# A PEER layer's first gathered rows brought into the query projection, with seven buffers that are free there

## The chip, the cores and the metric

The kernel runs on one core of one Trainium2 chip. The metric is device time in microseconds, the median of several runs. TensorE, VectorE, ScalarE, GpSimd and SyncE each run their own instruction stream and are ordered by semaphores alone; sixteen DMA engines move data between HBM and SBUF.

## The reference, cut to what matters

The program is two blocks on 256 tokens of width 2048 in float32. The first is a gated convolution with attention, the second a convolution and state-space mixer followed by a PEER layer (product-key retrieval of single-neuron experts) and a last norm. The change concerns the PEER layer:

```python
def peer(h, w_q, sub_keys, u_tab, v_tab):        # blocks of 128 tokens
        q = (xb @ w_q).reshape(128, 8, 2, 128)
        s = jnp.einsum('thcd,hcnd->thcn', q, sub_keys)
        s_top, i_top = lax.top_k(s, 16)
        cand = s_top[:, :, 0, :, None] + s_top[:, :, 1, None, :]
        best, pos = lax.top_k(cand.reshape(128, 8, 256), 16)
        expert = jnp.take_along_axis(cand_idx, pos, axis=-1)   # row of 16384
        gates = jax.nn.softmax(best, axis=-1)
        act = jax.nn.gelu(jnp.einsum('td,thkd->thk', xb, u_tab[expert]))
        return jnp.einsum('thk,thkd->td', gates * act, v_tab[expert])
```

Each token picks 8 heads x 16 = 128 experts, so each block of 128 tokens reads 128 x 128 rows of 2048 floats (8 KB) from each of two tables.

## The kernel before, in words

Everything ahead of PEER is a chain of projections. SyncE loads weight slabs of 1 MB into four buffers `weight_raw` (`load`, L276), each after the tile that last read the buffer, so four slabs ahead. TensorE multiplies tile by tile (`tile`, L381; `split_product`, L399, which uses the copies `weight_high`, `weight_low` and the operands `o_high`, `o_low` that lie over `operand`), and ScalarE or VectorE reads each tile out of PSUM.

**Query projection** (TensorE L618 to L629, ScalarE L907 to L914). Sixteen tiles, each 16 k-steps of two passes, from `op_b`. After each of tiles 0 to 3 TensorE turns four blocks (`M_TOK`, four transposes each, L622 to L627), which ScalarE copies out (L912): blocks 0 to 7 are the residual, into `y_tok`, and 8 to 15 the normed h, into `h_tok`. Two PSUM banks serve them in turn (`misc_bank`, L420). After the tiles of `SCORE_AFTER` (4, 5, 6, 8, 10, 12, 14, 15) TensorE makes one head's scores against the sub-keys (`head_scores`, L608), which ScalarE copies to `x_f` (`scores_out`).

**Picks** (VectorE). `head_picks` (L1417) finds the 16 best of each half, the 256 sums and the 16 best of these. `experts` (L1428) turns the positions of several heads into table rows and raises `picks_ready`; for block 0 it comes after heads 0 to 3, 4 to 6 and 7 (`HEAD_PARTS`). `softmax` (L1451) makes the gates, with the exponential on ScalarE (`softmax_exp`).

**Gathers** (GpSimd, L351 to L372). One indirect DMA brings one pick of 128 tokens: 128 rows of 8 KB, 1 MB, into one of eight buffers `rows` (two of `weight_raw`, six in `slots`; L202). GpSimd issues them in order: block 0's 128 of table u, its 128 of v, then block 1's, 512 in all, in rounds of eight buffers. Each waits until its buffer has been used (`row_free`), and the first for the last head's scores and the end of the projection (L362, L363).

**Dots and sums.** For table u VectorE multiplies each row with `h_tok` and adds it up (`dot_rows`, L1474). Then ScalarE makes the gelu and VectorE the weights `pick_w`. For table v the buffers with an odd number go to VectorE, which adds weight times row to `y_tok` (`add_rows`, L1489), and those with an even number to TensorE (L644), which multiplies them by a diagonal that ScalarE writes (L929), four products of 512 columns into PSUM. `add_sums` (L1493) joins both. `finish` (L1500) waits for ScalarE's square and root (L935, L937), scales by the gain, and SyncE stores (L320). VectorE picks block 1's heads in block 0's rounds of sums; block 1's `experts` and `softmax` stand ahead of the last round (L1515). The order on VectorE is written out at L1461 to L1466 and L1511 to L1527:

```python
            dot_rows(0)
            for i in range(ROUNDS):
                if i == ROUNDS - 1:
                    experts(1, 0, PEER_H)
                    softmax(1)
                if i < PEER_H:
                    head_picks(1, i)
                add_rows(0, i)
            add_sums(0)
            finish(0)
            dot_rows(1)
```

Of the kernel before, what the change touches and what calls it, by code (L numbers as in the profile page):

```python
# [33 lines left out]
HEAD_PARTS = ((0, 4), (4, 7), (7, 8))  # L34
SCORE_AFTER = [4, 5, 6, 8, 10, 12, 14, 15]
PICKS = PEER_H * PEER_K

# [83 lines left out]
def build(nc, d):  # L121
    ctx = ExitStack()
    with ctx:  # L123
# [7 lines left out]
        with nc.sbuf_tensor("weight_low", [P, NSLAB, SLAB], F32R) as w_low, \  # L131
                nc.sbuf_tensor("operand_low", [P, KD, T], F32R) as o_low, \
                nc.sbuf_tensor("operand_high", [P, KD, T], F32R) as o_high:
            pass
        w_raw = sb("weight_raw", [P, NSLAB, SLAB])
        opnd = sb("operand", [P, 2, KD, T])
        w_high = sb("weight_high", [P, NHIGH, SLAB], F32R)
# [64 lines left out]
        rows = [w_raw[:, n, :] for n in range(2)] + [slots_f[:, n * D:(n + 1) * D] for n in range(6)]  # L202
        ROWS = len(rows)
        ROUNDS = PICKS // ROWS
        PE_AT = range(0, ROWS, 2)
        DVE_AT = range(1, ROWS, 2)

# [50 lines left out]
        M_TOK = M_SUB + 4  # L258
        M_S = M_TOK + 16
# [67 lines left out]
        def _(pool):  # L327
# [23 lines left out]
            def gather(rnd, col0, table):  # L351

                for n in range(ROWS):
                    pool.wait_ge(row_free[n], rnd + 1)
                    nc.gpsimd.indirect_dma_start(  # L355
                        rows[n], None, table, bass.IndirectOffsetOnAxis(ap=picks[:, col0 + n:col0 + n + 1], axis=0),
                    ).then_inc(gathered[n], 16)

            for n in range(ROWS):
                pool.sem_inc(row_free[n], 1)  # L360

            pool.wait_ge(misc_done, M_S + PEER_H)  # L362
            pool.wait_ge(proj_done, TILES)  # L363
            per_head = PEER_K // ROWS
            for t in range(TT):
                for v, table in ((0, d["peer_u_2"][0]), (1, d["peer_v_2"][0])):
                    parts = [(*heads, n + 1) for n, heads in enumerate(HEAD_PARTS)] if t == v == 0 \
                        else [(0, PEER_H, len(HEAD_PARTS) + t)]
                    for first, last, ready in parts:
                        pool.wait_ge(picks_ready, ready)  # L370
                        for i in range(first * per_head, last * per_head):
                            gather(i + (2 * t + v) * ROUNDS, i * ROWS + t * PICKS, table)  # L372

# [4 lines left out]
        def _(pe):  # L378
# [229 lines left out]
            def head_scores(h):  # L608

                pe.wait_ge(proj_freed, freed(TILE_WQ + 2 * h + 2))  # L610
                bank = misc_bank(M_S + h, h == 0)
# [5 lines left out]

            pe.wait_ge(proj_freed, freed(TILE_WQ))  # L618
            for n in range(16):
                tile(TILE_WQ, n, op_b, ready=(lambda k: (h_scaled, 2 * KD + k + 1)) if n == 0 else None)  # L620

                for u in range(4 * n, 4 * n + 4 if n < 4 else 4 * n):  # L622
                    bank = misc_bank(M_TOK + u, u == 0)
                    src, t, g = (x_t, op_b)[u // 8], (u // 4) % 2, u % 4
                    for j in range(4):
                        tr = nc.tensor.transpose(bank[:, j * P:(j + 1) * P], src[:, 4 * g + j, t * P:(t + 1) * P], ident[:, :])
                    tr.then_inc(misc_done, 1)  # L627
# [5 lines left out]
            pe.wait_ge(misc_freed, M_S + 8)  # L633
            for t in range(TT):
# [4 lines left out]
                for i in range(ROUNDS):  # L639
                    for j, n in enumerate(PE_AT):  # L640
                        pe.wait_ge(diag_ready, (ROUNDS * t + i) * len(PE_AT) + j + 1)
                        pe.wait_ge(gathered[n], (i + (2 * t + 1) * ROUNDS + 1) * 16)
                        for c in range(4):
                            mm = nc.tensor.matmul(ps_v[:, c, :], diag[:, n, :], rows[n][:, c * 512:(c + 1) * 512],  # L644
                                                  start=False, stop=False, skip_group_check=True)
                        mm.then_inc(row_free[n], 1)
# [9 lines left out]
        def _(act):  # L656
# [244 lines left out]
            def scores_out(h):  # L901
                m = M_S + h
# [3 lines left out]

            for n in range(16):  # L907
                read_out(TILE_WQ, n, slot(n))
                for u in range(4 * n, 4 * n + 4 if n < 4 else 4 * n):
                    act.wait_ge(misc_done, M_TOK + u + 1)  # L910
                    dst, t, g = (y_tok, h_tok)[u // 8], (u // 4) % 2, u % 4
                    act_copy(dst[:, t, 512 * g:512 * g + 512], ps_m[:, (M_TOK + u) % 2, :]).then_inc(misc_freed, 1)  # L912
                if n in SCORE_AFTER:
                    scores_out(SCORE_AFTER.index(n))  # L914

# [5 lines left out]
            for t in range(TT):  # L921
# [3 lines left out]
                for i in range(ROUNDS):  # L925
                    for n in PE_AT:
                        at = i * ROWS + t * P + n
                        act.wait_ge(row_free[n], i + (2 * t + 1) * ROUNDS + 1)
                        nc.scalar.activation(diag[:, n, :], ident[:, :], ACT.Copy,  # L929
                                             scale=pick_w[:, at:at + 1]).then_inc(diag_ready, 1)  # L930
                if t == 0:
                    softmax_exp(1)
# [4 lines left out]
                nc.scalar.activation(out_sd[:, t:t + 1], out_ss[:, t:t + 1], ACT.Sqrt, bias=eps_c, scale=1.0 / D).then_inc(out_rooted, 1)  # L937

# [4 lines left out]
        def _(dve):  # L943
# [473 lines left out]
            def head_picks(t, h):  # L1417
                dve.wait_ge(misc_freed, M_S + h + 1)
# [42 lines left out]
            for h in range(PEER_H):  # L1461
                head_picks(0, h)
                for first, last in HEAD_PARTS:
                    if h == last - 1:
# [89 lines left out]
```

## Time and profile before

| | |
|---|---|
| median of 3 runs | 2709.89 us (2707.55 to 2713.97) |
| profiled execution, its span | 2704.8 us (it shows no other time of its own) |
| TensorE busy | 1845.0 us (68%) |
| VectorE busy | 1824.7 us (67%) |
| GpSimd busy | 903.3 us (33%) |
| ScalarE busy | 467.2 us (17%) |
| moved by DMA | 747.27 MB, of it 536.90 MB by the gathers |
| mean granted TensorE clock | 0.863 of full speed |

A slice of the page is a fortieth of the span, 67.6 us. The query projection lies at about 1271 to 1399 us and the gathers at 1401 to 2692. In the rows, PE is TensorE, PEld its weight load, DVE VectorE, ACT ScalarE, POOL GpSimd and SP SyncE; x16 is a count of instructions, and the brackets at a row's end hold the engine's idle time before it and what ended that.

### The profile page before, as it was taken

To read this page: it belongs to the slowest core of one execution; us is meant where nothing else is said; L and a number is where in the kernel's file an instruction comes from. 1 tells how busy PE (TensorE), PEld (TensorE's weight loads), DVE (VectorE), ACT (ScalarE), POOL (GpSimd) and SP (SyncE) were. 2 spreads that over 40 slices of the span, in tenths; PEclk is the share of its full clock that TensorE was granted. 3 is DMA by queue.
4 is the path that set the end of the run, shared out by engine and by line. 5 is a ranking of instruction groups with operands and counts; after the bars stand their busy time and mean duration, and the time that the engine had idled before them with its cause. 6 is when DMAs were issued, how large, how long until landed. Compare 5 with 4: busy or idle time off the path is not lost. (4 is left out here: it accounts for less than half of the span.)

```text
span 2704.8 us, 25287 instructions
## 1 busy us (share of the span) xinstructions
PE 1845.0 (68%) x9428; PEld 1434.6 (53%) x9428; DVE 1824.7 (67%) x2603; ACT 467.2 (17%) x737; POOL 903.3 (33%) x541
## 2 busy tenths in 40 slices
PE   7999999999999999999970000377772000067776
PEld 6999999987878888898860000122221000022222
DVE  5665676516868977254269999877449999954444
ACT  4345555401020101233110000000010000000001
POOL 2000000000000000000018888665556888855553
PEclk8999999998989999999995555699997555589999
DMA  6655555653535554465449999999999999999998
GB/s 161 186 166 162 166 162 156 172 140 105 148 91 156 140 155 141 140 187 155 126 149 422 422 422 422 422 421 421 422 422 382 422 422 422 421 422 422 422 421 338
DMA packets 458283, 747.27 MB, mean 276 GB/s; under 512 B 22130, under 2 KB 391236, under 8 KB 392260
## 3 DMA queue, kind: packets, MB, share of 16 engines
q0 software_dynamic: 73728, 536.90, 47.8%
q1 hardware_dynamic: 373248, 207.63, 27.2%
q10 hardware_dynamic: 11204, 1.29, 0.4%
q8 instruction: 74, 1.21, 0.2%
q14 instruction: 29, 0.24, 0.0%
HBM read 743.68 MB, written 2.10 MB: 276 GB/s over the span
## 5 line engine op out<-in xcount | busy, mean ns | idle before, releaser
L395 PE MATMUL ps<-operand,weight_raw 128*128 128x256 f32 x3072 | 674.7, 382 | 6.4 <-DVE operand L981 5.9
L395 PEld LDWEIGHTS ps<-operand,weight_raw 128*128 128x128 f32 x3072 | 588.1, 192 | 90.0 <-issue 8.4
L644 PE MATMUL ps<-weight_raw,residual_t 128*128 128x512 f32 x256 | 123.5, 627 | 677.2 <-ACT residual_t L929 637.4
L1474 DVE SCALAR_TENSOR_TENSOR slots<-slots,work 128x2048 f32<-128x2048 f32 x192 | 437.5, 2291 | 30.3 <-DMA slots<-in_peer_u,slots 29.9
L644 PEld LDWEIGHTS ps<-weight_raw,residual_t 128*128 128x128 f32 x256 | 48.2, 198 | 752.6 <-ACT residual_t L929 699.9
L644 PE MATMUL ps<-slots,residual_t 128*128 128x512 f32 x768 | 353.2, 603 | 119.0 <-DMA slots<-in_peer_v,slots 119.0
L355 POOL DMA_INDIRECT slots<-in_peer_u,slots x192 | 395.5, 2060 | 61.9 <-issue 58.6
L413 PE MATMUL ps<-operand_high,weight_high 128*128 128x256 f32 x1536 | 389.2, 293 | 10.5 <-POOL operand_low L337 6.4
L414 PE MATMUL ps<-operand_low,weight_high 128*128 128x256 f32 x1536 | 378.8, 286 | 0.0
L348 POOL IOTA slots<- 128x16 f32 x1 | 0.1, 146 | 1127.1 <-DVE operand L1387 1127.1
L1489 DVE SCALAR_TENSOR_TENSOR work<-slots,work 128x2048 f32<-128x2048 f32 x96 | 225.7, 2351 | 221.6 <-DMA slots<-in_peer_v,slots 221.2
L970 DVE TENSOR_TENSOR weight_low<-weight_raw,weight_high 128x2048 fp32r<-128x2048 f32 x96 | 220.6, 2298 | 159.2 <-ACT weight_high L658 158.6
L355 POOL DMA_INDIRECT slots<-in_peer_v,slots x192 | 261.6, 1362 | 183.8 <-PE ps L644 147.5
L644 PEld LDWEIGHTS ps<-slots,residual_t 128*128 128x128 f32 x768 | 139.1, 190 | 332.7 <-ACT residual_t L929 169.2
L413 PEld LDWEIGHTS ps<-operand_high,weight_high 128*128 128x128 f32 x1536 | 298.7, 194 | 17.9 <-issue 10.1
L414 PEld LDWEIGHTS ps<-operand_low,weight_high 128*128 128x128 f32 x1536 | 299.6, 195 | 2.2 <-issue 1.9
L355 POOL DMA_INDIRECT weight_raw<-in_peer_u,slots x64 | 133.6, 2087 | 273.0 <-PE ps L614 228.4
L658 ACT ACTIVATE weight_high<-weight_raw 128x2048 fp32r<-128x2048 f32 x96 | 183.2, 1909 | 116.5 <-PE ps L417 99.0
L417 PE MATMUL ps<-operand_high,weight_low 128*128 128x256 f32 x1536 | 201.6, 284 | 0.2 <-DVE weight_low L970 0.2
L417 PEld LDWEIGHTS ps<-operand_high,weight_low 128*128 128x128 f32 x1536 | 192.7, 193 | 0.4 <-DVE weight_low L970 0.4
L1474 DVE SCALAR_TENSOR_TENSOR weight_raw<-weight_raw,work 128x2048 f32<-128x2048 f32 x64 | 146.1, 2291 | 9.2 <-DMA weight_raw<-in_peer_u,slots 9.1
L711 ACT ACTIVATE slots<-ps 128x256 f32<-128x256 f32 x136 | 52.3, 384 | 563.1 <-PE ps L395 356.3
(209 smaller groups left out, 1508.8 us busy)
## 6 DMA issues: line engine op xcount, KB each, us to landing
weight_raw<-in_w_in SPq DMA_DIRECT2D x120, 1024.0 KB, 6.1
weight_raw<-in_w_out SPq DMA_DIRECT2D x32, 1024.0 KB, 5.9
weight_raw<-in_peer_w_q SPq DMA_DIRECT2D x16, 1024.0 KB, 5.8
weight_raw<-in_ssm_w_val SPq DMA_DIRECT2D x8, 1024.0 KB, 5.3
weight_raw<-in_ssm_w_gate SPq DMA_DIRECT2D x8, 1024.0 KB, 5.3
weight_raw<-in_conv_w_out SPq DMA_DIRECT2D x8, 1024.0 KB, 5.3
slots<-in_peer_u,slots POOLq DMA_INDIRECT x192, 16.4
slots<-in_peer_v,slots POOLq DMA_INDIRECT x192, 15.9
```

What stands on the lines that cost most here:

```text
L348: nc.gpsimd.iota(iota16, pattern=[[1, 16]], base=0, channel_multiplier=0, allow_small_or_imprecise_dtypes=True).then_inc(zero_ready, 1)
L355: nc.gpsimd.indirect_dma_start(rows[n], None, table, bass.IndirectOffsetOnAxis(ap=picks[:, col0 + n:col0 + n + 1], axis=0),).then_inc(gath ...
L395: mm = nc.tensor.matmul(ps_p[:, t % PSLOTS, :], w[:, k, :], operand[:, k, :], start=(k == order[0]), stop=(k == order[-1]))
L413: nc.tensor.matmul(out, high[:, k, :], o_high[:, k, :], start=(k == order[0]), stop=False)
L414: nc.tensor.matmul(out, high[:, k, :], o_low[:, k, :], start=False, stop=False)
L417: mm = nc.tensor.matmul(out, low[:, k, :], o_high[:, k, :], start=False, stop=(k == order[-1]))
L644: mm = nc.tensor.matmul(ps_v[:, c, :], diag[:, n, :], rows[n][:, c * 512:(c + 1) * 512], start=False, stop=False, skip_group_check=True)
L658: return nc.scalar.activation(dst, src, ACT.Copy)
L711: return nc.scalar.activation(dst, ps_p[:, n % PSLOTS, :], func, **kw).then_inc(proj_freed, 1)
L970: v.tensor_tensor(w_low[:, s % NSLAB, :], w_raw[:, s % NSLAB, :], w_high[:, i % NHIGH, :], ALU.subtract).then_inc(w_low_ready, 1)
L1474: v.scalar_tensor_tensor(out=rows[n], in0=rows[n], scalar=1.0, in1=h_tok[:, t, :], op0=ALU.mult, op1=ALU.mult, accum_out=dots[:, at:at + 1 ...
L1489: v.scalar_tensor_tensor(out=y_tok[:, t, :], in0=rows[n], scalar=pick_w[:, at:at + 1], in1=y_tok[:, t, :], op0=ALU.mult, op1=ALU.add).then ...
```

## The change

- `HEAD_PARTS` is now head 0, heads 1 to 3, heads 4 to 7; head 0's scores follow tile 1 and head 1's tile 4.
- TensorE turns blocks 0 to 7 ahead of tile 0, and the other eight two by two after tiles 1, 2, 3 and 5.
- There are eleven row buffers. Seven are free during the query projection: two in the place of `weight_high` (which now lies over a buffer `rows_high`), two in `op_a`, three in `slots`; the first 28 gathers go round in these. From gather 28 on, which waits for the end of the projection, the four of `weight_raw` join. `ROW[s]` and `USES[s]` are worked out for each of the 512 gathers, and the semaphore waits count by them.
- After `head_picks` of heads 0 to 6 VectorE dots 3, 4, 3, 3, 4, 3 and 4 rows, 24 in all (`DOTS_AFTER`), and the other 104 after `softmax(0)`.
- In block 0's sums VectorE picks head h of block 1 after pick 8h + 7, and makes `experts(1)` at pick 71. `softmax(1)` and `finish(0)` move into block 1's dots, after dots 12 and 8. On ScalarE `softmax_exp(1)` moves behind block 0's square and root.
- Odd and even go by pick and not by buffer, and the diagonals take sixteen places in turn.

```diff
-HEAD_PARTS = ((0, 4), (4, 7), (7, 8))
-SCORE_AFTER = [4, 5, 6, 8, 10, 12, 14, 15]
+HEAD_PARTS = ((0, 1), (1, 4), (4, 8))
+SCORE_AFTER = [1, 4, 6, 8, 10, 12, 14, 15]
+DOTS_AFTER = [3, 4, 3, 3, 4, 3, 4]
 PICKS = PEER_H * PEER_K
+EARLY_ROWS, MORE_ROWS = 7, 4
+ROWS = EARLY_ROWS + MORE_ROWS
+EARLY_PICKS = 4 * EARLY_ROWS
+def row_of(s):
+    if s < EARLY_PICKS:
+        return s % EARLY_ROWS
+    return (EARLY_ROWS + s - EARLY_PICKS) % ROWS
+ROW = [row_of(s) for s in range(4 * PICKS)]
+USES = [ROW[:s].count(ROW[s]) for s in range(4 * PICKS)]
...
-        rows = [w_raw[:, n, :] for n in range(2)] + [slots_f[:, n * D:(n + 1) * D] for n in range(6)]
-        ROUNDS = PICKS // ROWS
-        PE_AT = range(0, ROWS, 2)
-        DVE_AT = range(1, ROWS, 2)
+        rows_a = op_a.rearrange("p a b -> p (a b)")
+        rows = [rows_high[:, n, :] for n in range(2)] + [rows_a[:, n * D:(n + 1) * D] for n in range(2)] \
+            + [slots_f[:, n * D:(n + 1) * D] for n in range(3, 6)] + [w_raw[:, n, :] for n in range(MORE_ROWS)]
...
+            return (8, 9) if n == 1 else (10, 11) if n == 2 else (12, 13) if n == 3 else (14, 15) if n == 5 else ()
...
-            pool.wait_ge(misc_done, M_S + PEER_H)
-            pool.wait_ge(proj_done, TILES)
+            def gather(s, col, table):
+                b = ROW[s]
+                if USES[s] > 0:
+                    pool.wait_ge(row_free[b], USES[s])
+                nc.gpsimd.indirect_dma_start(
+                    rows[b], None, table, bass.IndirectOffsetOnAxis(ap=picks[:, col:col + 1], axis=0),
+                ).then_inc(gathered[b], 16)
             for t in range(TT):
...
+                        for i in range(first * PEER_K, last * PEER_K):
+                            s = (2 * t + v) * PICKS + i
+                            if s == EARLY_PICKS:
+                                pool.wait_ge(proj_done, TILES)
+                            gather(s, t * PICKS + i, table)
...
             pe.wait_ge(proj_freed, freed(TILE_WQ))
+            for u in range(8):
+                tokens(u)
             for n in range(16):
                 tile(TILE_WQ, n, op_b, ready=(lambda k: (h_scaled, 2 * KD + k + 1)) if n == 0 else None)
+                for u in tokens_after(n):
+                    tokens(u)
                 if n in SCORE_AFTER:
                     head_scores(SCORE_AFTER.index(n))
...
+                for i in range(0, PICKS, 2):
+                    if i >= 32:
+                        before = (2 * t + 1) * PICKS + i - 32
+                        act.wait_ge(row_free[ROW[before]], USES[before] + 1)
+                    nc.scalar.activation(diag[:, i // 2 % 16, :], ident[:, :], ACT.Copy,
+                                         scale=pick_w[:, t * P + i:t * P + i + 1]).then_inc(diag_ready, 1)
-                if t == 0:
-                    softmax_exp(1)
                 nc.scalar.activation(small[:, 52:53], eps_c, ACT.Sqrt)
...
+                if t == 0:
+                    softmax_exp(1)
...
+            done = 0
+            for h in range(PEER_H):
+                head_picks(0, h)
+                for first, last in HEAD_PARTS:
+                    if h == last - 1:
+                        experts(0, first, last)
+                if h < len(DOTS_AFTER):
+                    if h == 0:
+                        dve.wait_ge(misc_freed, M_TOK[11] + 1)
+                    for i in range(done, done + DOTS_AFTER[h]):
+                        dot_row(0, i)
+                    done += DOTS_AFTER[h]
+            softmax(0)
+            for i in range(done, PICKS):
+                dot_row(0, i)
+            weigh(0)
+
+            for i in range(1, PICKS, 2):
+                add_row(0, i)
+                if i % 8 == 7 and i // 8 < PEER_H:
+                    head_picks(1, i // 8)
+                elif i == 8 * PEER_H + 7:
+                    experts(1, 0, PEER_H)
+            add_sums(0)
+            sums_ready()
+            for i in range(PICKS):
+                if i == 8:
+                    finish(0)
+                elif i == 12:
+                    softmax(1)
+                dot_row(1, i)
+            weigh(1)
+            for i in range(1, PICKS, 2):
+                add_row(1, i)
+            add_sums(1)
+            sums_ready()
+            finish(1)
```

`dot_row(t, i)` and `add_row(t, i)` hold one turn each of the loops in the old `dot_rows` and `add_rows`, `weigh` the end of the old `dot_rows`, and `sums_ready` the first line of the old `finish`.

## Rows read from the trace of the kernel before

**Rows 1.** The page: GB/s of the 40 slices, and the gathers' DMA queue.

```profile
GB/s 161 186 166 162 166 162 156 172 140 105 148 91 156 140 155 141 140 187 155 126 149 422 422 422 422 422 421 421 422 422 382 422 422 422 421 422 422 422 421 338
...
q0 software_dynamic: 73728, 536.90, 47.8%
```

**Rows 2.** Windows: us, busy PE, PEld, DVE, ACT, POOL, granted clock, DMA share, GB/s.

```profile
1480.00:1600.00 120.00, 0.00 (x0) 0.00 (x0) 111.62 (x99) 0.00 (x0) 105.07 (x50) 0.50 1.01 422
...
1800.00:2000.00 200.00, 147.04 (x321) 57.49 (x320) 115.18 (x140) 16.06 (x40) 110.41 (x81) 1.00 1.01 422
```

**Rows 3.** Waits, 1250 to 2710: us in total, times, longest.

```profile
DVE slots L1408 <- ACT residual_t L658: 73.3, 7, 41.5
```

**Rows 4.** Windows of 2 us at the edges of the gathers.

```profile
1402.00:1404.00 2.00, 2.00 (x6) 0.83 (x5) 1.93 (x3) 0.44 (x1) 1.63 (x2) 1.00 0.63 168
...
2040.00:2042.00 2.00, 1.35 (x4) 0.28 (x2) 1.97 (x2) 0.00 (x0) 0.00 (x0) 1.00 0.31 131
...
2688.00:2690.00 2.00, 0.79 (x2) 0.49 (x3) 1.03 (x1) 0.00 (x0) 0.00 (x0) 1.00 0.41 172
```

**Rows 5.** Timeline of the query projection: start us, us, engine, line, operation.

```profile
1270.89 9.04 PE L395 MATMUL ps<-operand,weight_raw 128*128 128x256 f32 x32 [2.96 <-DVE operand L981]
...
1279.77 1.04 PE L626 MATMUL ps<-ident,residual_t 128*128 128x128 f32 x8
...
1281.75 1.08 ACT L658 ACTIVATE work<-ps 128x512 f32<-128x512 f32 x2 [0.26 <-PE ps L626]
...
1282.03 7.07 PE L395 MATMUL ps<-operand,weight_raw 128*128 128x256 f32 x32
...
1317.57 0.60 ACT L658 ACTIVATE residual_t<-ps 128x512 f32<-128x512 f32 x1 [0.51 <-PE ps L614]
...
1346.99 0.38 ACT L711 ACTIVATE slots<-ps 128x256 f32<-128x256 f32 x1 [6.52 <-PE ps L395]
...
1398.91 0.38 ACT L711 ACTIVATE slots<-ps 128x256 f32<-128x256 f32 x1 [6.31 <-PE ps L395]
```

**Rows 6.** Window of 1 us in tile 0; the last three columns as in rows 2.

```profile
1273.00:1274.00 1.00, 1.00 (x3) 0.75 (x3) 1.00 (x4) 0.00 (x0) 0.00 (x0) 0.50 0.00 0
```

**Rows 7.** Timeline of VectorE: picks, table rows, softmax and first dots.

```profile
1354.32 0.20 DVE L1434 TENSOR_SCALAR slots<-slots 128x64 uint32<-128x64 uint32 x1
...
1362.67 0.23 DVE L1448 SCALAR_TENSOR_TENSOR slots<-slots 128x64 uint32<-128x64 f32 x1
...
1405.27 0.48 DVE L1408 MAX8 slots<-residual_t 128x8 f32<-128x128 f32 x2
...
1411.02 0.37 DVE L1434 TENSOR_SCALAR slots<-slots 128x16 uint32<-128x16 uint32 x1
...
1414.59 0.28 DVE L1455 TENSOR_TENSOR slots<-slots 128x128 f32<-128x128 f32 x1
...
1416.14 2.29 DVE L1474 SCALAR_TENSOR_TENSOR weight_raw<-weight_raw,work 128x2048 f32<-128x2048 f32 x1
...
1418.36 2.29 DVE L1474 SCALAR_TENSOR_TENSOR weight_raw<-weight_raw,work 128x2048 f32<-128x2048 f32 x1
```

**Rows 8.** Timeline of GpSimd: the first gather and the eighth.

```profile
1400.79 1.32 POOL L355 DMA_INDIRECT weight_raw<-in_peer_u,slots  x1 [228.45 <-PE ps L614]
...
1410.46 0.94 POOL L355 DMA_INDIRECT slots<-in_peer_u,slots  x1 [0.30 <-issue]
```

**Rows 9.** Line 355, all gathers: from issue to landing.

```profile
DMA to landing us min/median/max: 5.7/16.3/17.5
```

**Rows 10.** The page's DMA issues: KB each, us to landing.

```profile
weight_raw<-in_peer_w_q SPq DMA_DIRECT2D x16, 1024.0 KB, 5.8
```

**Rows 11.** DMA queues in 1298 to 1316, two weight loads: records, MB, share.

```profile
q1 hardware_dynamic: 4128, 2.10, 43.2%
```

**Rows 12.** DMA queues in 2065 to 2071, gathers (q0) and the store (q1).

```profile
DMA packets 455, 2.55 MB, mean 425 GB/s; under 512 B 38, under 2 KB 38, under 8 KB 249
...
q0 software_dynamic: 228, 1.69, 66.6%
q1 hardware_dynamic: 227, 0.86, 35.1%
```

More of the change, by code:

```diff
@@ L638, in _ @@
                     nc.tensor.matmul(ps_v[:, c, :], zero_row[:, 0:P], zero_row, start=True, stop=False, skip_group_check=True)
[L639 to L646, printed above, removed]
+                for i in range(0, PICKS, 2):
+                    s = (2 * t + 1) * PICKS + i
+                    b = ROW[s]
+                    pe.wait_ge(diag_ready, (t * PICKS + i) // 2 + 1)
+                    pe.wait_ge(gathered[b], 16 * (USES[s] + 1))
+                    for c in range(4):
+                        mm = nc.tensor.matmul(ps_v[:, c, :], diag[:, i // 2 % 16, :], rows[b][:, c * 512:(c + 1) * 512],
+                                              start=False, stop=False, skip_group_check=True)
+                    mm.then_inc(row_free[b], 1)
                 for c in range(4):
@@ L1459, in softmax, with dot_row, weigh @@
                 own.do(v.tensor_tensor(g, g, head_rs.unsqueeze(2).broadcast_to([P, PEER_H, PEER_K]), ALU.mult))
[L1461 to L1464, printed above, removed]
-                        experts(0, first, last)
-            softmax(0)
-            def dot_rows(t):
-                for i in range(ROUNDS):
-                    for n in range(ROWS):
-                        at = i * ROWS + t * P + n
-                        dve.wait_ge(gathered[n], (i + 2 * t * ROUNDS + 1) * 16)
-                        v.scalar_tensor_tensor(out=rows[n], in0=rows[n], scalar=1.0, in1=h_tok[:, t, :], op0=ALU.mult,
-                                               op1=ALU.mult, accum_out=dots[:, at:at + 1]).then_inc(row_free[n], 1)
-                for n in range(ROWS):
-                    dve.wait_ge(row_free[n], (2 * t + 1) * ROUNDS + 1)
+            def dot_row(t, i):
+                s = 2 * t * PICKS + i
+                b, at = ROW[s], t * P + i
+                dve.wait_ge(gathered[b], 16 * (USES[s] + 1))
+                v.scalar_tensor_tensor(out=rows[b], in0=rows[b], scalar=1.0, in1=h_tok[:, t, :], op0=ALU.mult,
+                                       op1=ALU.mult, accum_out=dots[:, at:at + 1]).then_inc(row_free[b], 1)
+            def weigh(t):
+                for b in range(ROWS):
+                    dve.wait_ge(row_free[b], uses_before(b, (2 * t + 1) * PICKS))
                 v.tensor_copy(small[:, 48:49], small[:, 0:1]).then_inc(dots_ready, PICKS)
```

96 lines of the change are left out of this document (40 added, 56 removed).

## The prediction

> **What bounds the kernel now.** I read the page's slices and queues first [rows 1]: from the 22nd slice on the DMA engines move 422 GB/s almost without a pause, against 91 to 187 before it, and the gathers' queue carries 536.90 MB. Then the stages [rows 2]: in the dots (1480 to 1600) and in the sums (1800 to 2000) the DMA share is 1.01, while VectorE is busy for 112 of 120 and 115 of 200 us and TensorE for 0 and 147. So the second half is bound by bytes: 512 gathers of 536.90/512 = 1.0486 MB at 422 GB/s, 2.485 us each, 1272.3 us in all. No engine's work there is worth time; only bytes moved earlier, and pauses of the DMA engines, are. Both exist ahead of it: VectorE stands 73.3 us for scores in the projection [rows 3], and GpSimd 228.45 us before its first gather [rows 8].
>
> The fine windows [rows 4] give the edges. Row data starts near 1402.7 (share 0.63 in 1402 to 1404) and ends near 2688.9 (0.41 in 2688 to 2690): 1286.2 us. The rows take 1272.3; the last gain (1 MB) and block 0's store (1 MB), by their bytes, 2.5 us each; that leaves some 9 us of pause, most of it at the block boundary, where block 1's picks come late (share 0.31 in 2040 to 2042). From the last byte to the span's end it is 2704.8 - 2688.9 = 15.9 us, the last sum, the norm and the store, which the change leaves as they are.
>
> The span, 2704.8 us, is all that the profiled execution gives of its own time; the median of the runs is 5.1 us above it. All sums are made against the span, and 5.1 is added at the end. A measurement tells some 0.2% (5.4 us) from no change.
>
> **1. Turned blocks.** Eight of the sixteen now stand ahead of tile 0, where TensorE waits 2.96 us for the scaled operand [rows 5]. ScalarE, free after its root, copies a pair out per 1.35 us (1.09 and a wait of 0.26), so the four pairs take until about 1273. Tile 0 then starts 2 us later than before. But it took 9.04 us there, at a granted clock of 0.50 (1.2 GHz) in 1273 to 1274 [rows 6] after that wait, and a plain tile takes 6.9 (0.38 and a wait of 6.52): it ends near 1280 as before. The other eight come in pairs after tiles 1, 2, 3 and 5 at 1.04 us a pair, where two pairs, with the wait for ScalarE, took 2.26 (1279.77 to 1282.03). Four groups at 2.3 become four at 1.04: 5 us less. The last read-out, at 1398.9 before, would come at 1394.
>
> **2. Head 0's picks.** Its scores follow tile 1, so they are copied out at 1280 + 6.9 + 1.0 + 1.5 = 1289.4 (1.5 from the read-out at 1316.68 to the end of the copy at 1318.17). One head's picks take 5.75 us (1405.27 to 1411.02) and the table rows of 16 picks 3.57 (to 1414.59) [rows 7]: GpSimd starts gathering at 1298.7, 102 us sooner [rows 8]. The blocks of h_tok that the dots read (tokens 8 to 11) are out by 1298, so waiting for them costs nothing. A gather is issued per 1.24 us (0.94 and 0.30) and lands 5.7 us after its issue at the least [rows 9].
>
> **3. Rows against weights.** The query weights are loaded meanwhile, 5.8 us from issue to landing [rows 10], four slabs ahead, that is 4 x 6.9 = 27.6 us before TensorE needs one: 21.8 us of slack. Two loads are 4128 records and 43.2% of 18 us [rows 11]: 129 records per engine, 3.9 us, 0.03 us a record. A gathered row is 8 records per engine of 0.31 us. How do two queues share an engine? No stretch has such loads beside gathers; the nearest is block 0's store (4 KB records) among gathers: 228 records of one against 227 of the other [rows 12], turn by turn. Taking that for the weights, a waiting load gets one 0.03 us record for each 0.31 us record of a row, and 14 rows in a line let only 112 of its 129 pass. There is such a line: seven rows from 1298.7, three more as head 0's dots free buffers, four after head 1 (1321 to 1328) keep rows waiting from 1300.7 to 1300.7 + 14 x 2.72 = 1339. Tile 7's load, issued at 1304.7, then lands near 1343 instead of 1310.5, and TensorE, due at 1327.4, stands 15 us. The loads behind it catch up while no row can be issued (heads 1 to 3 are through near 1371); a second line, from row 16 on, costs under 1 us. The projection ends near 1409, not 1394. The other end of this price is 0: at equal time a load needs 2 x 3.9 us and keeps within its slack. I take the turn-by-turn value, since the only rows with both queues show it.
>
> **4. VectorE's order.** After heads 0 to 6 it dots 3, 4, 3, 3, 4, 3, 4 rows, 24 in all, at 2.22 us (1416.14 to 1418.36): 53 us, put where it stood 73. Queued behind each dot is the next head's picks. Head 7's scores are there at 1411; VectorE is in its dots until 1420, then 5.75 for the head, 8.6 for 64 picks' table rows (1354.32 to 1362.90) and 1.55 for the softmax: it is free for dot 24 at 1435.5. GpSimd passes row 28 only after the projection (1409), and row 35 needs dot 24's buffer. So rows up to 34 are in by 1435, dot 24 ends at 1437.7, and the next data flows 2.0 us later, at 1439.7 (1400.79 to 1402.7 before): a pause of 5 us.
>
> **5. The steady part.** Then 512 - 35 = 477 rows x 2.485 = 1185.3, plus 5.0 for gain and store: 2630.0. VectorE starts 11 rows behind and gains 0.27 us a row, and its rows wait in buffers: hidden. Eleven buffers instead of eight hold 27 us of transfers ahead, more than the 15 us of block 1's table rows, which now sit at pick 71, with the picks ready long before row 256: the pause at the boundary goes, and stays, up to 9 us, if that cover fails. The odd and even picks are the same work; sixteen diagonals run ahead of TensorE, hidden by the rows. Block 0's finish after dot 8 (2.5 us of VectorE and a wait for ScalarE) and the softmax after dot 12 put block 1's dots back by 5 us against 27 of cover: nothing. SP's store of block 0 moves back with it by 20 us and keeps its 2.5. The exp that now follows ScalarE's square and root has until dot 12. The new place of weight_high and the added semaphore counts change no access in the projection.
>
> **Sum.** 2630.0 + 15.9 = 2645.9 for the span, and 5.1 to the runs: **2651 us**, 59 less, 2.2%. As a ledger: 35 rows in by 1435 where it had 13, 22 x 2.485 = 55, less 5 of pause, plus 9 of the old pauses.
>
> **Rivals.** (A) is the forecast, chance 0.47. (B) The queues share so that no load comes late. Nothing stops before a load takes 21.8 us more. The projection ends at 1394, the picks are complete 10.4 us sooner, and everything follows: 2641. For it: these records are an eighth of the store's, and no row shows that a turn is one of them. The Trainium skill, "DMA: Bandwidth & Descriptors", section on queues, rings and completion order, says that an engine drains a whole packet, typically 9 to 17 descriptors, before it turns to the next ring; by that a load gets nine or more records a turn, and the sum would be B's. The trace's 228 against 227 does not decide it, since a 4 KB record may be a packet by itself. Chance 0.32.
> (C) VectorE loses more in the projection, each wait for a row or for a late head pushing all that follows. Its own work from 1298.7 to the last picks is 7 x 5.75 + 6.9 (48 picks, between 3.57 and 8.6) + 8.6 + 53 = 109, so 1408 without any wait; A has 26 of waits. With 20 more: 2671. Chance 0.09.
> (D) The early rows don't get through, stuck for buffers or a count: only the 5 us of blocks and 8 of the boundary remain, 2697. Chance 0.07, of it 0.02 within 0.2%.
> (E) Slower: half-kilobyte and 8 KB records together move at a much lower rate than either, so that the 28 early rows (69.6 us) and the twelve loads beside them (46) take far longer than 116 us. The 484 rows behind them, 1202.7 us, would lose the gain from a start at 1403 + 69.6 + 9 = 1482 on, 183 us after the first row: under 0.63 of the full rate the change loses, and at half the rate it gives 48 us more than before, 2758. Against it: store and gathers together moved 422 GB/s and more, 2.55 MB in 6 us [rows 12]. Chance 0.04. That leaves 0.01 for the unnamed.
>
> **The numbers.** Faster by over 0.2%: A, B, C and most of D, 0.94; same 0.02; slower 0.04. The range goes from 4 us under B (the end of the projection and the pauses are each known to a few) to above C: 2637 to 2674; A with a second tile late by the slack it lacks, 7 us, and a half clock after the stand, lies inside.
>
> **What would show it.** Right: gathers from about 1299; TensorE standing for one slab in 1327 to 1343 and that load's landing over 30 us (B: no such wait, landings near 10); 35 rows issued before dot 24, a DMA pause of 5 us near 1435 (B: 1425), none at the boundary, and 422 GB/s elsewhere. Wrong: a DMA share under 1 in the sums or dots, a pause at the boundary, or dots that stand for rows between the heads.

## The result, and the profile after

The changed kernel takes **2659.82 us** (2658.55 to 2660.46, 4 runs) against 2708.72 us (2707.14 to 2713.97, 4 runs) for the kernel before, measured in turn with it: a ratio of 0.9815, 95% interval 0.9803 to 0.9827, so 1.8% faster. The forecast was 2651 with a range of 2637 to 2674. The span of the profiled execution is 2658.2 us, where the forecast's sum had 2645.9: 12.3 us more. Of these, 3.5 do not show in the runs, because their median lies 1.6 us above the profiled span here and lay 5.1 above it before.

The page first: its line of GB/s and the gathers' queue. The 20th to 22nd slices, the query projection and what follows it, show 231, 301 and 330 where [rows 1] has 126, 149 and 422, and the dip at the boundary of the blocks (382 in [rows 1]) is gone.

```profile
GB/s 162 182 167 164 168 161 151 175 146 100 152 102 140 146 142 158 127 176 182 231 301 330 423 422 422 421 422 421 422 422 422 422 422 421 422 421 422 421 422 312
...
q0 software_dynamic: 73728, 536.90, 48.7%
```

Timeline of GpSimd, TensorE and ScalarE in the projection (start us, us, engine, line, operation, and in brackets the idle time before it with its releaser). The first gather starts at 1300.59, 100 us before that of [rows 8]. TensorE stands still for 15.91 us until tile 7's slab has landed (the projection's line is 425 here); tiles 7 and 8, joined in one row, take 16.31 us instead of 13.98 for such a pair later on. The last read-out is at 1413.43, 14.5 us later than in [rows 5].

```profile
1300.59 1.09 POOL L388 DMA_INDIRECT rows_high<-in_peer_u,slots  x1 [128.19 <-DVE slots L1489]
...
1345.16 16.31 PE L425 MATMUL ps<-operand,weight_raw 128*128 128x256 f32 x64 [15.91 <-DMA weight_raw<-in_peer_w_q]
...
1376.90 13.98 PE L425 MATMUL ps<-operand,weight_raw 128*128 128x256 f32 x64
...
1413.43 0.38 ACT L747 ACTIVATE slots<-ps 128x256 f32<-128x256 f32 x1 [6.31 <-PE ps L425]
...
1442.06 2.75 POOL L388 DMA_INDIRECT operand<-in_peer_u,slots  x1 [11.25 <-DVE operand L1507]
```

The load line (314), all weight loads, from issue to landing in us, minimum, median, maximum:

```profile
DMA to landing us min/median/max: 5.2/5.9/40.9
```

The loads of tiles 7, 8 and 9 landed 40.1, 40.9 and 29.8 us after their issue; the median of all loads, 5.9, is close to the 5.8 of [rows 10]. The reason shows in the DMA queues of 1315 to 1318 (queue, records, MB, share of the engines):

```profile
q0 software_dynamic: 153, 1.13, 92.1%
q1 hardware_dynamic: 154, 0.08, 9.1%
```

One record of a gathered row against one of the load, exactly as the store and the gathers took turns in [rows 12], though a row's record is 8 KB and the load's is 0.5 KB. The load moves a fourteenth of the rows' bytes (0.08 MB beside 1.13).

Windows (us; busy PE, PEld, DVE, ACT, POOL; granted clock, DMA share, GB/s), three places behind the projection where the DMA engines are not full, the block boundary, and the end:

```profile
1416.00:1418.00 2.00, 2.00 (x5) 0.83 (x5) 2.00 (x3) 0.96 (x1) 0.58 (x1) 1.00 0.43 176
1418.00:1422.00 4.00, 1.47 (x4) 0.38 (x2) 4.00 (x5) 0.00 (x0) 3.70 (x2) 1.00 0.27 59
...
1442.00:1446.00 4.00, 0.00 (x0) 0.00 (x0) 4.00 (x3) 0.00 (x0) 3.64 (x2) 0.50 0.20 39
...
1980.00:2060.00 80.00, 24.55 (x56) 10.26 (x56) 65.48 (x57) 5.17 (x6) 54.77 (x32) 0.72 1.01 422
2636.00:2638.00 2.00, 0.70 (x3) 0.29 (x2) 1.57 (x1) 0.00 (x0) 0.00 (x0) 1.00 0.86 360
2638.00:2640.00 2.00, 2.00 (x6) 0.80 (x6) 0.00 (x0) 0.00 (x0) 0.00 (x0) 1.00 0.24 98
2640.00:2644.00 4.00, 2.75 (x7) 1.02 (x6) 2.35 (x1) 0.00 (x0) 0.00 (x0) 1.00 0.06 27
```

The boundary's pause is gone. New is the end: the data of most engines is through near 2638, and from 2640 on the share is 0.06, which is one engine of sixteen (0.0625), until the last row is there at 2645. Before, the end was short: after the 0.41 of [rows 4] came

```profile
2690.00:2694.00 4.00, 3.67 (x15) 2.00 (x13) 2.35 (x2) 0.00 (x0) 0.00 (x0) 1.00 0.02 8
```

### The profile page after: what moved, and what is told of

Read it like the earlier page. It is cut to its first block and busy times, and to the rows that moved or that the text cites. A ratio compares the mean times of both kernels' runs of the same rounds, so it can differ in the third digit from the quotient of the medians.

```text
span 2658.2 us, 25285 instructions
## 1 busy us (share of the span) xinstructions
PE 1846.0 (69%) x9428; PEld 1435.7 (54%) x9428; DVE 1821.0 (69%) x2603; ACT 465.0 (17%) x737; POOL 897.5 (34%) x541
## 5 line engine op out<-in xcount | busy, mean ns | idle before, releaser
L425 PE MATMUL ps<-operand,weight_raw 128*128 128x256 f32 x3072 | 674.8, 382 | 19.3 <-DMA weight_raw<-in_peer_w_q 15.9
L680 PE MATMUL ps<-weight_raw,residual_t 128*128 128x512 f32 x368 | 172.2, 612 | 323.4 <-ACT residual_t L970 264.5
L680 PE MATMUL ps<-rows_high,residual_t 128*128 128x512 f32 x192 | 89.5, 609 | 344.1 <-ACT residual_t L970 316.0
L680 PEld LDWEIGHTS ps<-rows_high,residual_t 128*128 128x128 f32 x192 | 35.3, 193 | 398.2 <-ACT residual_t L970 346.1
L1507 DVE SCALAR_TENSOR_TENSOR weight_raw<-weight_raw,work 128x2048 f32<-128x2048 f32 x85 | 193.3, 2290 | 10.9 <-DMA weight_raw<-in_peer_u,slots 10.8
L388 POOL DMA_INDIRECT weight_raw<-in_peer_u,slots x85 | 170.8, 2009 | 29.4 <-issue 25.3
L1507 DVE SCALAR_TENSOR_TENSOR slots<-slots,work 128x2048 f32<-128x2048 f32 x75 | 170.4, 2289 | 8.1 <-DMA slots<-in_peer_u,slots 7.9
L1525 DVE SCALAR_TENSOR_TENSOR work<-weight_raw,slots,work 128x2048 f32<-128x2048 f32 x45 | 105.8, 2352 | 93.8 <-DMA weight_raw<-in_peer_v,slots 93.5
L388 POOL DMA_INDIRECT slots<-in_peer_u,slots x75 | 151.3, 2017 | 41.3 <-issue 21.9
L388 POOL DMA_INDIRECT weight_raw<-in_peer_v,slots x91 | 130.4, 1432 | 98.2 <-PE ps L680 71.8
L680 PE MATMUL ps<-slots,residual_t 128*128 128x512 f32 x272 | 126.2, 608 | 42.9 <-DMA slots<-in_peer_v,slots 42.9
```

The costliest lines, as they stand in the source:

```text
L388: nc.gpsimd.indirect_dma_start(rows[b], None, table, bass.IndirectOffsetOnAxis(ap=picks[:, col:col + 1], axis=0),).then_inc(gathered[b], 16)
L425: mm = nc.tensor.matmul(ps_p[:, t % PSLOTS, :], w[:, k, :], operand[:, k, :], start=(k == order[0]), stop=(k == order[-1]))
L680: mm = nc.tensor.matmul(ps_v[:, c, :], diag[:, i // 2 % 16, :], rows[b][:, c * 512:(c + 1) * 512], start=False, stop=False, skip_group_che ...
L1507: v.scalar_tensor_tensor(out=rows[b], in0=rows[b], scalar=1.0, in1=h_tok[:, t, :], op0=ALU.mult, op1=ALU.mult, accum_out=dots[:, at:at + 1 ...
L1525: v.scalar_tensor_tensor(out=y_tok[:, t, :], in0=rows[b], scalar=pick_w[:, at:at + 1], in1=y_tok[:, t, :], op0=ALU.mult, op1=ALU.add).then ...
```

## The experiments

The theory at this point: the gain is that of rows moved into the projection; what it lacks is TensorE's stand (turn by turn of records), the pause at 1442, and an end at which one late DMA engine is waited for. Each run is given against the kernel before, measured beside it (2708.7 to 2709.3), and against the 2659.82 of the changed kernel. The intervals of the ratios are up to 0.0014 either way, some 3.8 us; the times alone do not show a difference of 2 to 4 us, so each of these is told with the view that goes with it.

**1. No early rows.** All else stays.

```
-DOTS_AFTER = [3, 4, 3, 3, 4, 3, 4]
+DOTS_AFTER = []
...
-                            if s == EARLY_PICKS:
+                            if s == 0:
```

> The changed kernel, but GpSimd waits for the end of the query projection before gather 0 (not 28), and VectorE dots no row between the heads. Blocks, eleven buffers and the new block boundary stay. Theory (bytes moved early carry the gain): the projection ends near 1397 as no load competes, row data starts near 1399 instead of 1402.7, the pause at the boundary is gone; 512 rows x 2.485 + 5 = 1277 from there, then 16 to 20 us: span 2692 to 2697, so about 2695 us, 35 more than the changed kernel. Rival (the eleven buffers or the order in the steady part make the gain): within 5 us of 2660.

Measured: 2706.57 us, ratio 0.9987 (0.9978 to 0.9996), 12 us above the theory's 2695. So the early rows carry 47 of the 49 us; all that remains of the change is worth 2.5, not the 14 that steps 1 and 5 made it (5 for the blocks, 9 for the boundary), and the rival's 2660 is far off. The last read-out is at 1395.82, and TensorE waits for no slab: it is 3.1 us earlier than in [rows 5], where step 1 had 5. Row data starts at 1398.5, some 4 us earlier than in [rows 4]. Windows show where this head start goes: a pause after the seven early buffers are full, and the long end of one engine.

```profile
1416.00:1420.00 4.00, 0.00 (x0) 0.00 (x0) 4.00 (x5) 0.00 (x0) 3.20 (x2) 0.50 0.23 82
...
2682.00:2684.00 2.00, 1.25 (x3) 0.68 (x4) 0.59 (x1) 0.00 (x0) 0.00 (x0) 1.00 0.39 164
2684.00:2688.00 4.00, 2.76 (x7) 1.06 (x6) 2.35 (x1) 0.00 (x0) 0.00 (x0) 1.00 0.07 31
2688.00:2690.00 2.00, 2.00 (x6) 0.87 (x5) 0.00 (x0) 0.00 (x0) 0.00 (x0) 1.00 0.05 20
```

**2. The old boundary.** Block 0's finish ahead of block 1's dots, softmax (with its exponential on ScalarE) and table rows of block 1 at their old places.

```
             for i in range(1, PICKS, 2):
...
-                elif i == 8 * PEER_H + 7:
+                elif i == PICKS - 9:
                     experts(1, 0, PEER_H)
+                    softmax(1)
...
+            finish(0)
             for i in range(PICKS):
-                if i == 8:
-                    finish(0)
-                elif i == 12:
-                    softmax(1)
```

> The changed kernel with the old order around the block boundary: table rows and softmax of block 1 ahead of the last four sums, block 0's finish ahead of block 1's dots, the exponential ahead of the square. Theory (11 buffers do not help where the picks of block 1 are late; the pause of some 8 us at the boundary is part of the gain): a DMA pause of 4 to 9 us returns there, 2664 to 2669 us. Rival (eleven buffers alone cover it): no pause, 2660.

Measured: 2661.29 us, ratio 0.9820 (0.9807 to 0.9834). The pause is back, and the end is short again:

```profile
1996.00:2000.00 4.00, 2.71 (x7) 0.98 (x6) 3.49 (x7) 1.05 (x2) 0.94 (x1) 1.00 0.45 186
...
2640.00:2642.00 2.00, 1.99 (x5) 0.57 (x3) 1.24 (x1) 0.00 (x0) 0.00 (x0) 1.00 0.94 393
2642.00:2644.00 2.00, 0.72 (x2) 0.49 (x3) 1.11 (x1) 0.00 (x0) 0.00 (x0) 1.00 0.45 188
2644.00:2646.00 2.00, 2.00 (x6) 0.83 (x5) 0.31 (x1) 0.00 (x0) 0.00 (x0) 1.00 0.07 20
```

Most engines' data now ends 5 us later than in the changed kernel (2643 against 2638), the last row at about the same time. A pause in mid-stream is time in which the late engine catches up, so taking it away moves the others and hardly the end: 1.5 us by the medians, which the intervals don't tell from nothing. The semaphores show the catching up. Each row buffer's semaphore rises by 16 for a gather, once for each DMA engine, and the trace keeps the sixteen times. Here they lie 3.9 us apart for the last gather ahead of the pause (landed at 2000.9) and 1.5 us apart for the first behind it (2007.0); in the kernel before it was 5.0 (2044.9) and 1.7 (2051.1). The theory's number was too high. The rival's 2660 was met, but not by its mechanism: eleven buffers did not cover the old order, and the pause they left cost next to nothing.

**3. The turned blocks after tile 0.** Eight blocks stand behind tile 0 instead of ahead of it, so that tile 1 and head 0's scores are later.

```
-            return (8, 9) if n == 1 else ...
+            return range(8) if n == 0 else (8, 9) if n == 1 else ...
...
-            for u in range(8):
-                tokens(u)
```

> The changed kernel, but turned blocks 0 to 7 follow tile 0 instead of standing ahead of it. Theory: tile 0 starts at 1270.9 as before the change, is slow (9.0 us), and the eight blocks behind it cost ScalarE's pace, some 5.5 us; head 0's scores come 2 to 3 us later and so does all that follows, 2662 to 2663 us. Rival (the place of the blocks does not matter, since the stand for the weight load swallows it): 2660 within 1.

Measured: 2667.59 us, ratio 0.9851 (0.9837 to 0.9864), 7.8 us more where some 3 were expected. The first gather starts at 1306.49 instead of 1300.59, 5.9 later, and TensorE stands 17.1 us instead of 15.9, 1.2 more: that is 7.1 together. So the place of these eight blocks alone is worth more than the 5 us that step 1 gave to the whole new order, and the stand did not absorb the delay ahead of it.

**4. The rows held back for the slabs.** Gathers 3 to 15 wait for the projection, two more of them let through with each tile.

```
+                            if 3 <= s < 16:
+                                pool.wait_ge(proj_done, TILE_WQ + 3 + (s - 3) // 2)
```

> The changed kernel, but gathers 3 to 15 wait for tile 3 + (s - 3)/2 of the projection, two rows a tile, so that fewer rows stand in line while a weight load wants through. Theory (the 15.9 us stand of TensorE comes from rows and load records taking turns): a load then gets some 66 of its 129 records per tile time beside two rows and falls back by 2 us a tile, inside its slack: the stand shrinks from 15.9 to under 5 us, all behind it comes 5 us sooner, 2654 us. Rival 1 (the load is held back by something else, its own queue or HBM): the stand keeps its 16 us, 2660. Rival 2 (the stand costs nothing since the DMA engines work on): the stand shrinks and the time stays at 2660.

Measured: 2656.91 us, ratio 0.9809 (0.9796 to 0.9822); TensorE stands 12.1 us, not under 5. The stand fell by 3.8 us; the time fell by 2.9 by the medians, the way that was expected, but within the intervals. This brake was weak, and gathers 13 to 15 waited for tiles that were themselves late for their slabs: gather 13 was issued at 1350.70 after a wait of 20 us.

**5. Records of 1 KB for the query weights.** Each load brings 8 k-steps of 256 columns instead of 16 of 128, and tiles are made in pairs, half the k-steps at a time.

```
...
+                sp.dma_start(w_raw[:, at % NSLAB, :].rearrange("p (k n) -> p k n", n=256),
+                             w_q[:, 8 * h:8 * h + 8, 256 * q:256 * q + 256]).then_inc(raw_landed[at % NSLAB], 16)
...
```

> The changed kernel, but each load of query weights is 8 k-steps of 256 columns instead of 16 of 128: the same megabyte in 1024 records of 1 KB, 64 per engine; TensorE makes tiles in pairs by halves of k. Theory (an engine alternates record by record, whatever their size): a load needs 64 rows' records to pass instead of 129, 8 rows x 2.8 = 22 us at worst, about its slack of 21: landings fall from 40 us to 22 or less and the stand from 15.9 to 0 to 3 us; 2650 to 2655 us. Rival (shared by bytes or by time, or by packets of several records): the load's landing stays near 40 us or the record size changes nothing: 2660.

Measured: 2662.53 us, ratio 0.9826 (0.9812 to 0.9839). DMA queues in 1316 to 1320:

```profile
q0 software_dynamic: 200, 1.42, 86.1%
q1 hardware_dynamic: 202, 0.21, 14.8%
```

Still turn by turn, and the same number of turns now carries twice the bytes. So the turn is a record at each size that was seen beside the rows' 8 KB: 0.5, 1 and 4 KB. As a cure it failed: a pair of tiles needs two slabs at once, the two waits are 3.4 and 11.4 us, 14.8 together, and the projection ends no earlier. The expected time missed by 7 us or more for that reason.

**6. The last head after more dots.** Head 7's picks go behind six more dots, its table rows behind twelve, the softmax behind eighteen.

```
-            for h in range(PEER_H):
+            for h in range(PEER_H - 1):
...
-            softmax(0)
             for i in range(done, PICKS):
                 dot_row(0, i)
+                if i == done + 6:
+                    head_picks(0, PEER_H - 1)
+                if i == done + 12:
+                    experts(0, 4, 8)
+                if i == done + 18:
+                    softmax(0)
```

> The changed kernel, but after head 6 and its four dots VectorE goes on with six dots before head 7's picks, six more before the table rows of heads 4 to 7 and six more before the softmax, since gathers 35 to 63 need none of them. Theory (the pause near 1441 to 1446 exists because no buffer is given back while VectorE makes picks, table rows and softmax): the pause goes, row data flows on, up to 5 us less: 2655 us. Rival (the last DMA engine's lag sets the end, so that a pause of the other engines is worth little, as restoring the old boundary cost only about 1.5 us): the pause goes and the time stays within 2 us of 2660.

Measured: 2656.35 us, ratio 0.9810 (0.9796 to 0.9823), 3.5 us less by the medians, about what the theory expected, but within the intervals. The pause of 1442 is gone, the long end of one engine stays:

```profile
1442.00:1446.00 4.00, 0.00 (x0) 0.00 (x0) 3.93 (x6) 0.00 (x0) 3.57 (x2) 0.50 1.01 428
...
2632.00:2636.00 4.00, 2.70 (x7) 1.06 (x6) 1.80 (x1) 0.00 (x0) 0.00 (x0) 1.00 0.67 279
2636.00:2640.00 4.00, 2.77 (x7) 1.04 (x6) 2.35 (x1) 0.00 (x0) 0.00 (x0) 1.00 0.08 31
```

**7. Two slabs ahead of the rows.** The slabs of tiles 4 and 5 are loaded into two row buffers before any gather is issued, and each later load has six tiles to land instead of four. The gathers into these two buffers wait for the tiles.

```
+            for n in range(2):
+                sp.dma_start(slots_f[:, (3 + n) * D:(4 + n) * D].rearrange("p (k n) -> p k n", n=P),
+                             w_q[:, :, P * (4 + n):P * (5 + n)]).then_inc(ahead_in[n], 16)
-            for t in range(16):
+            for t in (0, 1, 2, 3) + tuple(range(6, 16)):
...
+                            if s in (5, 6):
+                                pool.wait_ge(proj_done, TILE_WQ + s)
```

> The changed kernel, but the weights of tiles 4 and 5 are loaded ahead of the projection into two of the seven row buffers (they become the sixth and seventh, and gathers 5 and 6 wait for those tiles); every later load is issued six tiles ahead instead of four, 41 us instead of 27.6. Theory (TensorE stands because a load beside rows takes up to 40 us): no stand, the projection ends near 1398 instead of 1413, and all behind it comes about 10 us sooner: 2650 us. Rival (VectorE's dots and picks set the pace, not TensorE): the stand goes and the time stays within 3 us of 2660.

Measured: **2646.90 us**, ratio 0.9774 (0.9760 to 0.9787), 12.9 us below the changed kernel and 3 below what was expected. Waits of TensorE (in total, times, longest):

```profile
PE ps L435 <- DMA weight_raw<-in_peer_w_q: 5.3, 1, 5.3
```

10.6 of the 15.9 us of stand are gone, where the theory had all of them gone, and the last tile starts at 1395.95 instead of 1406.32, 10.4 us earlier. The end came 12.9 us earlier, so at least all that TensorE gained reached it. (Two gathers are held back as well, as in run 4.)

**8. Both.** Run 7 with run 6's order of VectorE.

> Both edits of the two kernels before this one: two slabs ahead and the last heads' work late. Theory: the two gains add up, 10 + 5, about 2645 us. Rival (the slowest DMA engine limits): not below 2650.

Measured: 2647.10 us (2641.95 to 2647.74), ratio 0.9771 (0.9758 to 0.9785): nothing beyond run 7, where 2 us were expected, and below the rival's 2650. The profile is that of the 2641.95. The stand is 3.0 us and there is no pause behind the softmax, but one where the projection ends (run 7 has that one too):

```profile
1400.00:1404.00 4.00, 2.75 (x15) 1.89 (x14) 3.96 (x4) 1.81 (x3) 1.07 (x1) 1.00 0.05 20
1404.00:1408.00 4.00, 2.97 (x7) 0.95 (x5) 4.00 (x5) 0.46 (x1) 3.59 (x2) 1.00 0.42 104
```

**9. The four weight buffers released one by one.** Run 8, but the gathers into them wait for tiles 13, 14, 15 and 16, instead of all for the last, and take the buffers in the order in which they come free.

```
-                            if s == EARLY_PICKS:
-                                pool.wait_ge(proj_done, TILES)
+                            if EARLY_PICKS <= s < EARLY_PICKS + 4:
+                                pool.wait_ge(proj_done, TILES - 3 + s - EARLY_PICKS)
```

> The kernel ahead_and_late, with the four buffers of w_q released one by one: the gathers into them wait for projection tiles 13, 14, 15 and 16 instead of all for the last. There the DMA share fell to 0.39 in 1400 to 1410 us, some 6 us of engine time. Theory (the gathers run without a gap from 1299 on, and any gap before 1410 moves the whole train of rows): the gap goes and the time falls by 4 to 6 us, to about 2642. Rival 1 (the slowest DMA engine sets the end, and it used the gap to catch up, as at the block boundary): the gap goes but the last row lands no more than 1 to 2 us earlier, 2645 to 2647. Rival 2 (VectorE cannot free buffers earlier, so the gap turns up again behind the softmax): a gap at 1430 to 1450, 2647.

Measured: 2645.16 us, ratio 0.9762 (0.9748 to 0.9775), the fastest kernel of the study but not to be told from runs 7 and 8. The gap did not go, and it was none of the four buffers that it waited for. GpSimd's timeline:

```profile
1396.06 0.94 POOL L392 DMA_INDIRECT slots<-in_peer_u,slots  x1 [0.30 <-issue]
1405.50 2.75 POOL L392 DMA_INDIRECT slots<-in_peer_u,slots  x1 [8.49 <-DVE slots L1517]
1408.55 1.91 POOL L392 DMA_INDIRECT weight_raw<-in_peer_u,slots  x1 [0.30 <-issue]
```

It stands 8.49 us for a dot: VectorE first waits 2.27 us for head 6's scores and then picks for 5.7 us (1397.22 to 1402.93) before it dots again. The gather ahead of the four is one of the seven buffers that turn. So with the stand gone VectorE's stretch between dots is the next bound, as rival 2 had it in kind, though in front of the softmax and not behind it.

**10. Three slabs ahead.** Run 9 with a third slab, tile 6's, in a row buffer, loaded once TensorE has turned the sub-keys, which stood in its place; gathers 4 to 6 wait for tiles 4 to 6.

> As the run before, with a third slab of w_q loaded ahead into a row buffer, so that later loads have seven tiles to land. Theory (what is left of TensorE's stand, some 3 us, goes, and the projection ends 3 us earlier): 1 to 3 us below the run before, about 2640. Rival (the projection's end no longer decides once the buffers are released one by one; VectorE's picks and softmax do): the same as the run before within 1 us. If the extra prefetch takes bandwidth from the first tiles, tile 0 is late and it is 3 to 5 us slower.

Measured: 2647.37 us, ratio 0.9767 (0.9754 to 0.9781): no gain, a miss against 2640, and 2.2 us above run 9, which the intervals don't tell apart. The first gather is at 1306.62 instead of 1302.34, so the front is late, as the last sentence on record allowed. The waits for slabs are 4.6 and 1.6 us, not none, and the last tile starts 6.4 us later than in run 9 (1402.76 against 1396.39). In 1300 to 1310 the DMA share is 0.54: three of the seven buffers wait for tiles, and transfer time is left unused.

**11. Eight buffers.** The changed kernel with one of the four weight buffers instead of all.

```
-EARLY_ROWS, MORE_ROWS = 7, 4
+EARLY_ROWS, MORE_ROWS = 7, 1
```

> The changed kernel with eight row buffers instead of eleven. Theory (the eleven buffers are the cover for VectorE's stretches of several us without dots: softmax, experts, the end of block 0): the DMA pauses come back behind the softmax and at the block boundary, 8 to 12 us together, of which the slowest engine's catching up gives back up to 5, so 2663 to 2672. Rival (any pause lets the slowest engine catch up and is given back whole): no more than 2661.

Measured: 2668.49 us, ratio 0.9856 (0.9842 to 0.9869), 8.7 us more, as the theory had it; the rival's 2661 falls. Most of the cost stands behind the softmax: GpSimd now waits 14.98 us for dot 24, against 11.25, and the DMA share is low for some 11 us, against 3. At the block boundary, where a pause was expected too, none is seen. A short one stands where VectorE makes block 1's table rows, now in the sums, and GpSimd waits 11.34 us for the next sum; the late engine caught up there too (the sixteen landings 4.2 us apart before, 0.6 after).

```profile
1430.00:1440.00 10.00, 0.00 (x0) 0.00 (x0) 9.25 (x15) 1.47 (x2) 0.00 (x0) 0.50 0.43 182
1440.00:1450.00 10.00, 0.00 (x0) 0.00 (x0) 10.00 (x9) 0.12 (x1) 6.78 (x4) 0.50 0.42 154
...
1890.00:1892.00 2.00, 0.31 (x1) 0.30 (x2) 1.97 (x2) 0.00 (x0) 1.70 (x2) 1.00 0.19 74
```

## Why the prediction was right, and where it was off

The direction, the mechanism and the chain that rival A described are what the trace shows: gathers from 1300.59 (forecast 1298.7), one stand of TensorE of 15.91 us (15) up to 1345.16 (1343), landings near 40 us, a pause before row 35's data, none at the boundary, 421 to 422 GB/s from there to near 2638. B, C, D and E are out. The gain was 49 us of the 59 forecast; by the spans alone it would have missed by 3.5 us more, and that these do not show is luck (last point below). B, no stand, fell by the 153 against 154 records; with it falls, for this pair of queues, the rule of the Trainium skill, "DMA: Bandwidth & Descriptors", section on queues, rings and completion order, by which a whole packet of typically 9 to 17 descriptors is drained before the next ring has its turn. The trace disagrees with it at 0.5 and 1 KB beside 8 KB.

Point by point:

**Step 1, the blocks:** the last read-out is at 1395.82 in run 1, which has no stand, against 1394: 3.1 us gained, not 5. Run 3 puts 7.8 us on the place of the first eight blocks, a price that step 1 does not give apart.

**Step 2, head 0's picks:** 1.9 us late, about as much as tile 0 (1273.97 against 1273) and what follows it take.

**Step 3, rows against weights:** right, and shown by the records of 154 and 153 and by runs 5 and 7. What it left out of the sum, though it named it for the range, is the clock: TensorE stood 16 us, then had a granted clock of 0.53 in 1345 to 1350 (nearly all of it at 1.2 GHz), and its tile pair took 2.3 us more. By an estimate 1.6 us of that would have been a second stand at full clock, since tile 8's slab landed only at 1353.7, 8.5 us after tile 7 began, and a tile at full clock takes 6.9. With it, the 0.9 us of stand and the later start, the last read-out was 4.4 us late (1413.4 against 1409).

**Step 4, VectorE's order:** row 35's data came at 1444.9, not 1439.7. 4.4 of the 5.2 us are the projection's, and 0.8 is GpSimd's own: this gather took 2.75 us to issue beside a dot, where step 4 used the 2.0 us from the first gather to data of [rows 8] and [rows 4].

**Step 5, the steady part:** from 1444.9 to the end of most engines' data near 2638 are 1193, against 1190.3: 2.7 us more. This part was right, but the sum then added 15.9 us to it, the time from the last byte to the end as it was before. That term was too small: with one engine behind the others, the end of most engines' data is not the end of the train. It measured 20.3 us, 4.4 more. And the credit for the boundary, which the forecast's ledger counts as 9 us, was worth 1.5 by the medians (run 2), since the old pause was also time in which that engine caught up.

5.2 + 2.7 + 4.4 give the 12.3 of the span.

**From the span to the runs:** the 5.1 us that the forecast added came from one profiled span beside the median of other runs. In every run whose own span is known the time lies only 1.8 to 2.4 us above it. So this term was too large, and it covered part of the error by luck.

That one engine makes the long end is read from the share of a sixteenth there, from run 2, in which a pause shortens it, and from the sixteen times of the rows' semaphores: at the end the last of them stands 5.3 us behind the one before it. No view here names the engine. What makes the 2.7 us is open.

## What to carry to other kernels

When a bulk stream of long records is moved beside loads of short ones, count records and not bytes: the short loads get one turn for each long record, so load ahead of the stream what is needed during it, as run 7 did for 13 us. Before a pause of a saturated resource is booked as a gain, ask whether it lets something that is behind catch up: read the DMA share after the last full window, not only the pause. And once the transfers reach into a stage, the longest stretch in which the consumer frees no buffer is the next bound, whatever frees the other buffers.

## What the runs showed of the hardware that was not expected

**One of the sixteen DMA engines falls behind in steps.** At the end of a train of some 500 rows without a pause the share is 0.05 to 0.08, about a sixteenth: in 2640 to 2644 in the changed kernel, 2684 to 2690 in run 1, 2636 to 2640 in run 6. Spread over 1190 us such a lag looks like an engine that is 0.5% slower. It is not: between steps this engine keeps pace. The time by which the last of a gather's sixteen landings is behind the one before it grows by 0.1 us in the 150 us from 2088 to 2238 (3.05 to 3.18). It then goes from 3.18 to 4.16 us from one gather to the next (landed at 2242.9 and 2246.4), and between these two stands one record of another queue, in 2243 to 2246:

```profile
q0 software_dynamic: 174, 1.25, 101.6%
q14 instruction: 1, 0.01, 0.7%
```

Five steps of 0.9 to 1.0 us, each at such a record of 8 KB (at 1804.0, 1906.8, 2083.8, 2244.0 and 2498.6), make 4.8 of the 5.3 us at the end. Two other records of this queue in that time (2008.2 and 2326.8) go without a step, and the trace does not say on which engine any of them ran. All runs show such steps, run 1 six of them. That the records cause the steps is argued from the times alone; no run takes them away, and why 8 KB, 0.3 us by themselves, should cost 1 us is open. The Trainium skill, "DMA: Bandwidth & Descriptors", section on latency and other measured facts, states that engines 7 and 15 are usually slower than the others, with the port of the software descriptor ring as its best guess of a cause. The trace agrees that one engine ends behind the others, but in steps; which one it is, no run here shows.

**A turn is one record at 0.5, 1 and 4 KB** against 8 KB: 154 to 153, 202 to 200, and 227 to 228 [rows 12].

**GpSimd's issue of a gather** takes 0.94 us, but 1.91 beside VectorE's dots and up to 2.99 in the projection. So after a pause the rows start again at one per 2.21 us (1.91 and 0.30), little faster than the 2.485 at which they move.
